# Moving six waits in a streaming encoder step: a log store, a pooling buffer, conversions and tile rows

## The reference, cut to what matters

```python
h = rmsnorm(x, g_mix_pre)
q, k, v, f, u, ga, gb = split(h @ w_in)            # f: 16 columns, u: 1024
logf = log_sigmoid(f + b_f)                        # an output too
a_out = forgetting_attend(q, k, v, cumsum(logf))   # samples: with 256 cached keys
pooled = trailing_mean(u, windows 2, 4, 8, 16) - u # four groups of 256 channels
m = sigmoid(ga) * (a_out @ w_attn_up) + sigmoid(gb) * (pooled @ w_pool) * pool_scale
x = x + rmsnorm(m @ w_out, g_mix_post)
z = square(relu(rmsnorm(x, g_ffn_pre) @ w_ff1))
y = x + rmsnorm(z @ w_ff2, g_ffn_post)
```

## Time and profile before

| what | value |
|---|---|
| median of 3 runs | 1975.76 us (1972.59 to 1976.14) |
| the profiled execution | 1979.12 us, its span 1977.5 us |
| TensorE matmul / weight load busy | 1935.3 us (98%) / 1784.6 us (90%) |
| VectorE, ScalarE, GpSimd busy | 853.1 (43%), 660.7 (33%), 190.4 us (10%) |
| mean granted TensorE clock | 0.992 |
| DMA | 269.45 MB, mean 136 GB/s |

### The profile page before, as it was taken

One profiled execution on the slowest core, in us unless ns is written; L12 is line 12 of the kernel. 1 busy time (PEld: TensorE's weight loads), 2 busy tenths in 40 slices (PEclk: granted clock), 3 DMA queues, 4 the chain that ended last, 5 costly groups with the idle time before them and its releaser, 6 DMA issues.

```text
span 1977.5 us, 26730 instructions
## 1 busy us (share of the span) xinstructions
PE 1935.3 (98%) x10594; PEld 1784.6 (90%) x10594; DVE 853.1 (43%) x1119; ACT 660.7 (33%) x932; POOL 190.4 (10%) x243
## 2 busy tenths in 40 slices
PE   8997999999999999999999999999999999999997
PEld 7997999989999998887989889899898898998986
DVE  5653444434333324446443434434434444444446
ACT  4333433433223323335323323223233232232332
POOL 1452332320000102000000000000000000000000
PEclk9998999999999999999999999999999999999999
DMA  7356878855434436423444344343443444434432
GB/s 203 121 139 160 185 174 165 183 148 128 128 125 128 124 127 221 160 86 113 132 128 128 128 127 126 127 126 127 128 127 128 127 128 128 126 127 127 126 127 83
DMA packets 210321, 269.45 MB, mean 136 GB/s; under 512 B 15329, under 2 KB 138433, under 8 KB 209312
## 3 DMA queue, kind: packets, MB, share of 16 engines
q1 hardware_dynamic: 194912, 235.98, 41.4%
q0 software_dynamic: 15296, 31.90, 5.3%
HBM read 260.69 MB, written 7.08 MB: 135 GB/s over the span
## 4 chain that ended last, share of the span: by engine, by line
PE 92%; DVE 2%; DMA 2%; POOL 1%; issue 1%; ACT 1%; DVEq 0%; SPq 0%; ACTq 0%; POOLq 0%
PE ps L492 18%; PE ps L493 18%; PE ps L494 18%; PE ps L519 11%; PE ps L518 11%; PE ps L520 11%; PE ps L669 1%; DMA out_dram<-logf_nat 1%; PE ps L735 0%; PE ps L686 0%; DVE w_lo L1447 0%; DMA bias_s<-ncs_dram 0%; DMA ncs_dram<-ncs 0%; PE ps L740 0%; PE ps L657 0%
## 5 line engine op out<-in xcount | busy, mean ns | idle before, releaser
L1447 DVE TENSOR_TENSOR w_lo<-w_raw,w_hi 128x1024 fp32r<-128x1024 f32 x426 | 531.9, 1250 | 829.4 <-ACT w_hi L1003 826.3
L1003 ACT CAST w_hi<-w_raw 128x1024 fp32r<-128x1024 f32 x426 | 446.5, 1050 | 870.8 <-PE ps L494 438.6
L492 PE MATMUL ps<-ht_hi,w_hi 128*128 128x384 f32 x2000 | 675.7, 338 | 5.2 <-DVE ht_lo L1492 3.4
L494 PE MATMUL ps<-ht_hi,w_lo 128*128 128x384 f32 x2000 | 669.4, 335 | 0.0
L493 PE MATMUL ps<-ht_lo,w_hi 128*128 128x384 f32 x2000 | 669.4, 335 | 0.0
L492 PEld LDWEIGHTS ps<-ht_hi,w_hi 128*128 128x128 f32 x2000 | 376.3, 188 | 6.5 <-DVE ht_lo L1492 3.6
L493 PEld LDWEIGHTS ps<-ht_lo,w_hi 128*128 128x128 f32 x2000 | 376.5, 188 | 1.8 <-issue 1.4
L494 PEld LDWEIGHTS ps<-ht_hi,w_lo 128*128 128x128 f32 x2000 | 376.2, 188 | 0.0
L518 PE MATMUL ps<-w_hi,z_hi 128*128 128x512 f32 x762 | 298.9, 392 | 1.8 <-DVE w_lo L1447 1.8
L519 PE MATMUL ps<-w_lo,z_hi 128*128 128x512 f32 x762 | 300.5, 394 | 0.0
L520 PE MATMUL ps<-w_hi,z_lo 128*128 128x512 f32 x762 | 295.9, 388 | 0.0
(11 more groups left out here) (274 smaller groups left out, 1310.7 us busy)
## 6 DMA issues: line engine op xcount, KB each, us to landing
w_raw<-in_w_ff_dram SPq DMA_DIRECT2D x256, 512.0 KB, 3.7
w_raw<-in_w_in_dram SPq DMA_DIRECT2D x130, 512.0 KB, 7.7
w_raw<-in_w_out_dram SPq DMA_DIRECT2D x32, 512.0 KB, 5.0
kc<-in_cache_k_dram POOLq DMA_DIRECT2D x8, 1024.0 KB, 11.1
vc<-in_cache_v_dram POOLq DMA_DIRECT2D x8, 1024.0 KB, 9.6
w_raw<-in_w_attn_up_dram SPq DMA_DIRECT2D x16, 512.0 KB, 3.7
bias_s<-ncs_dram POOLq DMA_DIRECT2D x64, 48.0 KB, 6.7
out_dram<-z_gain SPq DMA_DIRECT2D x6, 512.0 KB, 2.7
```

What stands on the lines that cost most here:

```text
L492: pe.matmul(out, wh[:, k, cols], x_hi[:, kk, :], start=(kk == 0), stop=False)
L494: last = pe.matmul(out, wl[:, k, cols], x_hi[:, kk, :], start=False, stop=(kk == k_last))
L1003: nc.scalar.copy(w_hi[:, u % RING, :], w_raw[:, u % RAWS, :]).then_inc(hi_ready, 1)
L1447: nc.vector.tensor_tensor(w_lo[:, u % RING, :], w_raw[:, u % RAWS, :], f32(w_hi[:, u % RING, :]), ALU.subtract).then_inc(lo_ready, 1)
```

## The change

Six edits. (1) GpSimd issues the two logf_nat stores behind the last windows, ahead of the stores of the pool rows, and ScalarE's three waits move into head pair 1, ahead of turned_prompt. (2) WIN_FLIP swaps the two sum buffers for step 3, so its first level waits for pooled of step 1 only and its second for pooled of step 2. pool_lo is split into pool_diff and pool_lo, and pool_diff(2), pool_diff(3) go ahead; on ScalarE slot(U_POOL) goes between the last two pool_inputs. (3) group_hi(6), group_hi(7), group_lo(6), group_lo(7) go behind the conversions of units 152 and 153, the table load behind that of unit 157. (4) turned_hi(1, 0) goes ahead of y_square(3, 2), and turn_h(1, 3) waits for one square less. (5) turned_hi and turned_lo of tile row 1 go ahead of conversions, x2 and its squares. (6) In the last chunk the last two conversions (units 436 and 437) go ahead of the evictions of cg 2.

```diff
@@ TensorE
-                    pe.wait_ge(ssq_ready[1], 1 + 3 * TT + g)
+                    pe.wait_ge(ssq_ready[1], 3 + 3 * TT)
@@ ScalarE, pooling
             pool_input(ORDER[2])
+            slot(U_POOL, 0)
             pool_input(ORDER[3])
...
-                slot(U_POOL + s, 0)
+                if s >= 1:
+                    slot(U_POOL + s, 0)
@@ ScalarE, head_pair
                     exp_sample(a, 1)
+                    if not later(a):
+                        act.wait_ge(pool_stored, 144)
+                        act.wait_ge(nc_stored, 144)
+                        act.wait_ge(logf_stored, 32)
                     turned_prompt(a)
...
             head_pair(U_HP, 0, 0, 0, False)
-            act.wait_ge(pool_stored, 144)
-            act.wait_ge(nc_stored, 144)
-            act.wait_ge(logf_stored, 32)
@@ ScalarE, output projection
-            group_hi(6)
-            group_hi(7)
             act.sem_inc(ssq_ready[1], 1)
-            nc.scalar.activation(root_warm[:, :], var[:, 0, :], ACT.Sqrt)
...
                 kept_slot(U_OUT + n)
+                if n < 2:
+                    group_hi(6 + n)
+                elif n == 5:
+                    nc.scalar.activation(root_warm[:, :], var[:, 0, :], ACT.Sqrt)
@@ ScalarE, tile rows
+            turned_hi(1, 0)
             y_square(3, 2)
-            turned_hi(1, 0)
             kept_slot(U_FFN - 1)
             root(1, 2)
             turned_hi(1, 1)
             kept_slot(U_FFN)
+            turned_hi(1, 2)
             kept_slot(U_FFN + 1)
-            x2_square(2)
             kept_slot(U_FFN + 2)
-            turned_hi(1, 2)
-            root(2, 2)
             kept_slot(U_FFN + 3)
             turned_hi(1, 3)
+            x2_square(2)
             kept_slot(U_FFN + 4)
+            root(2, 2)
             kept_slot(U_FFN + 5)
@@ ScalarE, chunk (VectorE alike)
-                        slot(n + 16 + 4 * cg + q, more)
+                        if not (is_last and cg == 3 and q < 2):
+                            slot(n + 16 + 4 * cg + q, more)
                     if is_last:
+                        if cg == 2:
+                            slot(n + 28, more)
+                            slot(n + 29, more)
@@ VectorE, pooling
-            def pool_lo(s, g):
+            def pool_diff(s, g):
                 w = 2 << g
-                fin = g % 2
+                fin = (g + WIN_FLIP[s]) % 2
...
                                         ALU.subtract).then_inc(pooled_ready, 1)
+
+            def pool_lo(s, g):
                 dve.wait_ge(pl_hi_ready, s + 1)
...
             slot(U_POOL, 0)
+            pool_diff(2, ORDER[2])
             outs(0, ORDER[0])
             pool_lo(2, ORDER[2])
...
+            pool_diff(3, ORDER[3])
             slot(U_POOL + 2, 0)
             pool_lo(3, ORDER[3])
@@ VectorE, output projection
-            group_lo(6)
-            group_lo(7)
...
                 kept_slot(U_OUT + n)
+                if n < 2:
+                    group_lo(6 + n)
@@ VectorE, tile rows
             kept_slot(U_FFN)
+            turned_lo(1, 2)
             kept_slot(U_FFN + 1)
+            kept_slot(U_FFN + 2)
             x2(2)
-            kept_slot(U_FFN + 2)
-            turned_lo(1, 2)
+            kept_slot(U_FFN + 3)
+            turned_lo(1, 3)
             var_x2(2)
-            kept_slot(U_FFN + 3)
+            kept_slot(U_FFN + 4)
             norm_rstd(2, 2, 3, 3)
-            turned_lo(1, 3)
-            kept_slot(U_FFN + 4)
             normed(2)
@@ GpSimd, windows
+                flip = WIN_FLIP[s]
                 if s >= 1:
-                    pool.wait_ge(pooled_ready, s)
+                    pool.wait_ge(pooled_ready, s - flip)
...
                         pool.wait_ge(win_level, levels[0])
+                        if flip:
+                            pool.wait_ge(pooled_ready, s)
-                    dst = lev % 2
+                    dst = (lev + flip) % 2
...
             windows(3, ORDER[3])
+            pool.wait_ge(fnat_saved, 1)
+            pool.dma_start(lfp_v, logf_nat[:, 0:2, :]).then_inc(logf_stored, 16)
+            pool.dma_start(lfs_v, logf_nat[:, 2, :]).then_inc(logf_stored, 16)
             pool.wait_ge(unat_saved, 4)
...
             load_bias(0)
-            pool.wait_ge(fnat_saved, 1)
-            pool.dma_start(lfp_v, logf_nat[:, 0:2, :]).then_inc(logf_stored, 16)
-            pool.dma_start(lfs_v, logf_nat[:, 2, :]).then_inc(logf_stored, 16)
```

More of the change, by code:

```diff
@@ L43 @@
 ORDER = (3, 2, 0, 1)
+WIN_FLIP = (0, 0, 0, 1)
 DFF = 4 * D
@@ L1622, in _ @@
             slot(U_UB + 3, 0)
+            pool_diff(0, ORDER[0])
             pool_lo(0, ORDER[0])
@@ L1632, in _ @@
             slot(U_UB + 5, 0)
+            pool_diff(1, ORDER[1])
             pool_lo(1, ORDER[1])
@@ L2006, in chunk @@
                     for q in range(4):
-                        slot(n + 16 + 4 * cg + q, more)
+                        if not (is_last and cg == 3 and q < 2):
+                            slot(n + 16 + 4 * cg + q, more)
+                    if is_last and cg == 2:
+                        slot(n + 28, more)
+                        slot(n + 29, more)
                     for t in range(TT):
@@ L2073, in windows @@
                 pool.wait_ge(u_saved, 2 * s + 2)
+                flip = WIN_FLIP[s]
                 if s >= 1:
-                    pool.wait_ge(pooled_ready, s)
+                    pool.wait_ge(pooled_ready, s - flip)
                 for lev in range(g + 1):
                     d, lo = 1 << lev, (2 << lev) - 1
-                    src_p = u_p[:, 2 * g:2 * g + 2, :] if lev == 0 else win_p[:, (lev - 1) % 2, :, :]
+                    src_p = u_p[:, 2 * g:2 * g + 2, :] if lev == 0 else win_p[:, (lev - 1 + flip) % 2, :, :]
                     if lev >= 1:
                         pool.wait_ge(win_level, levels[0])
-                    dst = lev % 2
+                        if flip:
+                            pool.wait_ge(pooled_ready, s)
+                    dst = (lev + flip) % 2
                     nc.gpsimd.tensor_tensor(win_p[:, dst, :, lo:], src_p[:, :, lo:],
@@ L2084, in windows @@
                     for c in range(2):
-                        src_s = u_s[:, 2 * g + c, :, :] if lev == 0 else win_s[:, (lev - 1) % 2, c, :, :]
+                        src_s = u_s[:, 2 * g + c, :, :] if lev == 0 else win_s[:, (lev - 1 + flip) % 2, c, :, :]
                         last = nc.gpsimd.tensor_tensor(win_s[:, dst, c, :, lo:], src_s[:, :, lo:],
```

## The result

| | before | after |
|---|---|---|
| median of 4 runs | 1974.3 us (1972.59 to 1976.14) | 1961.04 us (1959.77 to 1961.51) |
| profiled execution / its span | 1979.12 / 1977.5 us | 1961.18 / 1959.6 us |
| mean granted TensorE clock | 0.992 | 0.996 |

The ratio is 0.9927, 95% interval 0.991 to 0.9943: faster by 0.7%. The forecast was 1957.5 in a range of 1952 to 1966. From profiled execution to profiled execution the gain is 17.9 us, where the sum of the terms was 18.3. From median to median it is 13.3.

The account below looks back on a forecast made before the run. TensorE, busy 98% of the span, was taken as the bound, gains coming only from its idle and half-clock stretches. Terms -12.6 + 0 - 1.2 - 2.8 - 1.7 = -18.3 us off the median 1975.76 gave 1957.5, range 1952 to 1966.

Parts of the forecast that it names:

- Part A: Log-forget store, 155 to 173 us: moving it removes TensorE's 10.9 us gap and 1.7 us at half clock, -12.6.
- The lower end: Log-forget store: unit 33 lands at 169.8, wanted near 170.5; if loads fall behind, the gain shrinks to about 8 us.
- The step to the median: The -18.3 us sum gives 1960.8 on the profiled execution's own time; taken off the median instead, 1957.5.
- Part B: Pooling stage: 4.5 us offered, booked 0 because TensorE would wait for unit 29's load before rows_back; ends 0 and -4.5.
- C: Output projection: unit 152's conversion no longer stands behind group conversions and table load, the 1.24 us gap goes, -1.2.
- D: Tile rows at the first FFN units: 0.4 us plus 2.4 us of gaps go, -2.8; ends -1.0 and -4.1.
- E: Last chunk: TensorE gains 3.5 us at unit 436, but the end moves only with VectorE's finishes, -1.7; ends 0 and -3.5.
- R2: Rival, 0.16: the wait of some 4.8 us before rows_back drops the clock to 0.50, losing 1 to 1.7 us; 1958.9.
- R1: Rival, 0.15: the pooling gain is kept because unit 29 lands some 4 us earlier; -22.8, 1953.0.
- R5: Rival, 0.04: the moved wait still blocks because another store lands late; only output, tile-row and last-chunk gains remain, 1970.
- R3: Rival, 0.08: units 33 to 35 land late in head pair 1, 4 to 5 us come back; 1962.
- R4: Rival, 0.03: weight supply fails in all seven pairs, making it slower; 3.3 us a pair ends at 1980.6.

Follow-up runs that it names:

- before again: The kernel before, run once more with no edit: 1978.42 us, ratio 1.0008; its profiled execution took 1969.34 us.
- A alone: Kernel before with only the logf_nat stores moved behind the last window sum and ScalarE's three waits moved: 1966.47 us, ratio 0.9951.
- A and B undone: Changed kernel with the log-forget store edit and the pooling edit both undone: 1971.28 us, ratio 0.997.
- B undone: Changed kernel with the pooling edit alone undone: 1960.33 us, ratio 0.9913.
- changed again: Changed kernel, run once more with no edit: 1963.5 us, ratio 0.9926.
- outs(0) first: Changed kernel with outs(0) ahead of pool_diff(2) on VectorE again, cache loads left in place: 1961.59 us, ratio 0.9927.
- values later: Changed kernel with the first load of cached values (1 MB) moved behind the attention bias of head pair 0: 1959.55 us, ratio 0.9907.
- best version: Changed kernel with the cached values loaded behind the bias and outs(0) ahead of pool_diff(2) on VectorE: 1957.88 us, ratio 0.99.
- B undone, values later: Changed kernel with the pooling edit undone and the cached values loaded behind the bias: 1959.5 us, ratio 0.9918.

## Why the prediction was right, and where it was not

**The bound and the order of the stretches:** right. Every gap named was TensorE's, and each went with the edit that was said to remove it.

**Part A:** -12.4 against -12.6 between the two profiled executions. No wait on logf_nat, no gap, clock 1.00 at 172. The lower end was not needed: unit 33 landed at 168.64 and nobody waited for it.

**The step to the median** failed: "The profiled execution took 1979.12 us, its span 1977.5; that is 3.4 above the median of 1975.76", and the sum was then taken off the median. On its own time the sum gave 1960.8, and the profiled execution of the changed kernel took 1961.18. But what made the execution read long was, as the second trace of the kernel before shows, above all the wait that part A removes. An excess that lies inside a removed term goes with the term. Measured, A is worth 10.3 us by the medians, 2.1 us less than the 12.4 between the profiled executions, so some 2.1 of the 3.4 us were taken off twice, and the median would have been forecast at 1959.6 (an estimate, since the chips differ). The 1.4 us left to 1961.04 are near what part B cost. The rest of the 3.4 us fits the median of three runs having been low: the groups of 9 to 23 runs gave 1976.72 to 1977.92. Part A's term should have had the landing's scatter in it as a lower end; one execution does not show it, but the median of 1975.76 and the lowest run of 1972.59 beside 1979.12 were a sign of it.

**The sum:** that 1960.8 and 1961.18 are only 0.4 us apart is in part luck. Part B's +1.6, booked at 0, was nearly made up by 0.8 us more than booked from C, D and E, and by 0.5 us from a gap in the FFN loop that the change does not touch.

**Part B** failed: booked at 0, between 0 and -4.5, it came out at +1.6 between the profiled executions. Against the run without it, it cost 3.2 us by the medians, 2.1 in one trace, and gained 0.3 in the other. Two steps of it are wrong.

- That "the cache loads that share them only move forward with the rest" was read as harmless. They moved forward by 1.6 us while the load of unit 28 did not (its issue went from 117.85 to 117.72). The table has, for each run, the issue of unit 28, then how long after it the cache's keys and values were issued, and how long after it the unit landed.

| run | unit 28 issued | keys, later by | values, later by | landed, later by |
|---|---|---|---|---|
| before | 117.85 | 16.3 | 17.5 | 25.9 |
| before again | 118.77 | 16.0 | 17.2 | 25.6 |
| A alone | 119.05 | 16.1 | 17.3 | 28.0 |
| A and B undone | 118.01 | 16.3 | 17.5 | 27.1 |
| B undone | 118.21 | 16.4 | 17.5 | 27.2 |
| changed | 117.72 | 14.9 | 16.1 | 31.3 |
| changed again | 119.13 | 15.0 | 16.2 | 30.1 |
| outs(0) first | 118.02 | 14.9 | 16.1 | 30.8 |
| values later | 118.55 | 15.0 | 37.3 | 25.9 |
| best version | 118.90 | 14.9 | 36.5 | 25.8 |
| B undone, values later | 118.34 | 16.0 | 37.3 | 26.3 |

With keys and values 1.0 to 1.5 us sooner behind it the unit lands 2.1 to 5.7 us later; with the values out of the way it lands at the old 26 us, though the keys are as early. That the place of the values makes the difference is shown by "values later" and "best version" (and by the three runs with one part taken out of the best version, 25.8 to 26.2). Why 1.0 to 1.5 us of lead cost up to 5 is open: at their old place the values cost some 2 us at most (25.6 to 28.0 against 26.3).

- Passing outs(0) was not priced at all: "That difference moves ahead of outs(0) on VectorE" stands there without a term. It was 1.45 us of work by the kernel before, and 3.1 us beside the window sums that the same edit starts sooner.

The wait of about 4.8 us before rows_back did not come; it was 2.78 us, one unit earlier. The rival R2 (the moved wait costs clock) was the mechanism that occurred: 0.50 from 151.2 to 154.6 behind that wait, 0.50 behind outs(0) in two other runs. Against it the prediction had set the gap of 1.74 us alone; the 2.10 us at 911 had brought none either (clock 1.00 from 908 to 912), one more reason against R2, and it came all the same. The bounds should have had an end above zero.

**Parts C, D and E:** -1.4, -3.1 and -2.0 against -1.2, -2.8 and -1.7 in the traces, and each comes back when it is undone (0.9 to 2.1, 2.5 to 4.0, 1.6 to 2.8 us). The residues were where they were said to be: 1.28 us at the first FFN unit ("about 1.3"), 0.46 at unit 184 ("0.4"), and VectorE without a pause at the end. E gained 0.3 more because the finishes also came 5.37 us apart and not 5.5.

**The rivals:** R1 and R5 fell (no earlier landing of unit 29, no wait on the stores), R3 and R4 too: the DMA share in the head loop is 0.80 and TensorE waited for no weight unit from pair 1 on.

## What to carry to other kernels

When a wait ends on a DMA, its price in one trace is a sample: look at a second execution before you subtract it, and when the profiled execution is longer than the median, ask which stretch holds the excess, for if it is the stretch that you remove, the excess is gone with it and must not be taken off the median again. A gain ahead of a load that is nearly late can be given back at its landing, and a transfer that the edit moves forward can hold that load up, as 1 MB of values did here, so price the transfers that move as you price the instructions. Before an instruction is put ahead of another on one engine, look at what the neighbouring engine will be doing at its new time.

## What the runs showed of the hardware that was not expected

**A small store beside weight loads.** The log store, 16 KB and then 8 KB, landed 4.03, 3.94 or 11.43 us after its second issue from the same place in the program, with weight loads running beside it in each case. At its new place 11 executions had 12.7 to 14.4 us. What makes the difference at the old place no run here shows.

**VectorE beside GpSimd.** The same instruction on 128 x 241 floats took 0.39 to 0.41 us alone and 1.28 us when it started at 107.01, 0.07 us into a window sum of 1.08 us (106.94 to 108.02). It ended 0.27 us behind that sum. The Trainium skill, "SBUF — State Buffer", section "SBUF: two separate sides", says that VectorE and GpSimd share a pair of ports under a lock, so that a VectorE instruction with two inputs in SBUF waits for a running GpSimd instruction that reads SBUF and does not merely slow down. The trace agrees within 0.13 us: the rest of the sum (1.01 us) and the 0.40 us of the instruction make 1.41, and it took 1.28. The third of the six comes out alike: started at 108.80 beside a sum that ended at 109.32, it took 0.79, where 0.52 and 0.40 make 0.92.

**The clock behind short gaps.** Behind 1.96 us at outs(0) it fell to 1.2 GHz in two runs (from 112.5 and from 111.6) and stayed at 2.4 GHz in the changed kernel's profiled execution. Behind the 1.74 us at the first FFN unit, where the kernel before had kept 1.00, it was 0.50 from 889.9 in the second execution of the same kernel. Over all traces it fell behind the 2.0 us of the pooling stage in five of six executions, behind the 1.79 us of the last chunk in two of four, behind the 1.74 us in one of four, and behind the 2.10 us at the fifth FFN unit, the longest of these, in none of three. So a gap of about 2 us may or may not cost another 1.7 us, its length alone doesn't tell, and neither does one trace.
